# Gated delta rule scan: two steps' triangular inverses in one pass, a state kept in two buffers, and per-head scaling operations

## What is computed

```python
def gated_delta_scan(q, k, v, g, beta, s0):
    ...
    decay = jnp.exp(jnp.where(tril, gcum[..., :, None] - gcum[..., None, :], -jnp.inf))
    kb = kc * bc[..., None]
    lower = jnp.where(strict, jnp.einsum('nbhid,nbhjd->nbhij', kb, kc) * decay, 0.0)
    rhs = jnp.concatenate([vc * bc[..., None], kb * jnp.exp(gcum)[..., None]], axis=-1)
    sol = lax.linalg.triangular_solve(eye + lower, rhs, left_side=True, lower=True, unit_diagonal=True)
    u, w = sol[..., :dv], sol[..., dv:]
    attn = jnp.where(tril, jnp.einsum('nbhid,nbhjd->nbhij', qc, kc) * decay, 0.0)
    def step(S, inp):
        q_i, k_i, u_i, w_i, a_i, g_i = inp
        v_new = u_i - jnp.einsum('bhck,bhkv->bhcv', w_i, S)
        o = (jnp.einsum('bhck,bhkv->bhcv', q_i * jnp.exp(g_i)[..., None], S)
             + jnp.einsum('bhij,bhjv->bhiv', a_i, v_new))
        g_last = g_i[..., -1]
        S = (S * jnp.exp(g_last)[..., None, None]
             + jnp.einsum('bhck,bhcv->bhkv', k_i * jnp.exp(g_last[..., None] - g_i)[..., None], v_new))
        return S, o
```

## Time and profile before

| | us |
|---|---|
| median of 3 runs | 4184.54 (4180.77 to 4185.28) |
| span of the profiled execution | 4178.0 |
| first scan, 214.2 to 418.7 | 204.5 |
| second scan, 574.9 to 776.5 | 201.6 |
| TensorE busy over the span | 3781.0 (90%) |
| VectorE / ScalarE / GpSimd busy | 2122.6 / 870.5 / 398.1 |

### The profile page before, as it was taken

One profiled execution on the slowest core, in us unless ns is written; L12 is line 12 of the kernel. 1 busy time (PEld: TensorE's weight loads), 2 busy tenths in 40 slices (PEclk: granted clock), 3 DMA queues, 4 the chain that ended last, 5 costly groups with the idle time before them and its releaser, 6 DMA issues. The chain is left out here.

```text
span 4178.0 us, 67184 instructions
## 1 busy us (share of the span) xinstructions
PE 3781.0 (90%) x28350; PEld 2477.1 (59%) x28350; DVE 2122.6 (51%) x4187; ACT 870.5 (21%) x2114; POOL 398.1 (10%) x506
## 2 busy tenths in 40 slices
PE   7988989995999979899899598897989999999998
PEld 3477467772444435565677244334358878468877
DVE  3777677555222215576646433333464455564455
ACT  3144134411000002251621100002230001441001
POOL 0033013100111110150600000000000000000000
PEclk9999999997999989899999799998999999999999
DMA  7500520027999971211411799994112222122221
GB/s 250 179 27 12 182 92 18 21 82 278 392 392 393 402 262 41 91 52 41 142 61 61 296 405 405 410 421 156 41 66 81 71 91 96 41 94 93 71 91 56
DMA packets 166940, 674.20 MB, mean 161 GB/s; under 512 B 13480, under 2 KB 26984, under 8 KB 142064
## 3 DMA queue, kind: packets, MB, share of 16 engines
q1 hardware_dynamic: 155232, 650.89, 40.7%
q0 software_dynamic: 9984, 16.78, 1.8%
q10 hardware_dynamic: 1424, 2.23, 0.2%
HBM read 652.85 MB, written 17.02 MB: 160 GB/s over the span
## 5 line engine op out<-in xcount | busy, mean ns | idle before, releaser
L3756 PE MATMUL bank<-weight_ring_extra_b,xs_b 128*32 128x512 f32 x2544 | 281.8, 593 | 2.4 <-DMA weight_ring_extra_b<-in_moe_in 2.4
L3756 PE MATMUL bank<-weight_ring,xs_b 128*32 128x512 f32 x1936 | 219.7, 604 | 11.7 <-DVE xs_b L3859 6.1
L3848 ACT ACTIVATE moe_silu_b<-bank 128x256 f32<-128x256 f32 x80 | 25.5, 383 | 957.5 <-PE bank L3756 957.5
L2865 PE MATMUL bank<-heads_out_b,swiglu_sums_b 128*128 128x256 f32 x1008 | 224.4, 379 | 0.0
L3859 DVE TENSOR_SCALAR xs_b<-bank,factor_b,mod_b 128x64 f32<-128x64 f32 (+1 forms) x384 | 95.4, 323 | 228.3 <-PE bank L3740 228.3
L2865 PEld LDWEIGHTS bank<-heads_out_b,swiglu_sums_b 128*128 128x128 f32 x1008 | 191.5, 190 | 26.0
L3756 PEld LDWEIGHTS bank<-weight_ring_extra_b,xs_b 128*32 128x32 f32 x2544 | 79.1, 110 | 178.4 <-issue 173.3
L3813 PE MATMUL bank<-weight_ring_extra_b,moe_hidT_b 128*32 128x256 f32 x2784 | 161.5, 391 | 12.0 <-DMA weight_ring_extra_b<-in_moe_down 10.4
L1776 POOL TENSOR_TENSOR d_level_b<-d_low_b,d_mask_b 128x256 f32<-128x256 f32 x144 | 115.9, 833 | 544.2 <-DVE d_far_b L2035 542.4
L3900 DVE TENSOR_TENSOR heads_out_b<-heads_out_b,bank 128x256 f32<-128x256 f32 x256 | 90.2, 415 | 151.1 <-PE bank L3793 151.1
L2249 PE MATMUL bank<-hT_b,token_block_sums_b 128*128 128x256 f32 x608 | 145.1, 393 | 15.7 <-DVE hT_b L2383 15.7
(11 more groups left out here) (618 smaller groups left out, 7699.6 us busy)
## 6 DMA issues: line engine op xcount, KB each, us to landing
weight_ring_extra_b<-in_moe_in SPq DMA_DIRECT2D x60, 2048.0 KB, 23.8
weight_ring<-in_moe_in SPq DMA_DIRECT2D x48, 2048.0 KB, 24.5
weight_ring_extra_b<-in_moe_down SPq DMA_DIRECT2D x33, 2048.0 KB, 25.0
weight_ring<-in_ada_w SPq DMA_DIRECT2D x24, 2048.0 KB, 8.1
weight_ring<-in_moe_down SPq DMA_DIRECT2D x21, 2048.0 KB, 25.1
weight_ring<-in_ssd_w_in SPq DMA_DIRECT2D x12, 2048.0 KB, 8.2
hT_b<-in_moe_in SPq DMA_DIRECT2D x10, 2048.0 KB, 41.9
weight_ring<-in_ffn_w_gate SPq DMA_DIRECT2D x10, 2048.0 KB, 7.8
```

Of the source, the lines that this page charges most:

```text
L2865: last = pe.matmul(out, lhs[:, k, :], rhs[:, k, :], start=(k == 0), stop=(k == HK - 1))
L3756: last = pe.matmul(in_bank(g)[lanes[c], :], xs[:, e % 2, kt, g * GROUP:(g + 1) * GROUP], w[:, k, :, c * COLS:(c + 1) * COLS], start=(kt == 0),
L3848: last = act.activation(sl[:, g, :], in_bank(g)[:, 0:COLS], ACT.Silu)
```

## The change

Steps are taken in pairs. Both inverses of a pair are built in one pass: `L`, `far`, `A`, `UW`, `U` and `C` have a further axis `j` for the two steps, and every instruction of a level covers both. At size 64 the transpose is done by 64x64 products with the identity. What is waited for before the pass is now the `L` of both steps, and so their decays and Grams. To find room, slots 0 and 2 of the weight ring are lent to the scan until the last pair's inverse is done (`gdn_lent`), and only then are they loaded for the following stage.

`S` has two buffers, so a step reads the old one while the new one is written, and `state` goes ahead of `o` on TensorE. The right side becomes `V * beta` on GpSimd (`values`) and one scalar_tensor_tensor per head on VectorE (`right`), and the state one scalar_tensor_tensor per head (`renew`). The scaled keys move to ScalarE, by one activation per head (`fade_keys`). All Grams are copied to SBUF and two of each direction are made inside the first pair's levels (sizes 8 and 32).

```diff
+        later = {8: s + 2, 32: s + 3}.get(size, TT)
...
+                pool.tensor_tensor(R[:, d], V[:, t], wide(dec.beta, d, t), ALU.mult).then_inc(pom[d].sem, 1)
...
+                wait(pool, dvm[d], s + 1, "low")
+                pool.tensor_tensor(small(A[:, d, n % 2]), small(L[:, d]), over_small(mask[:, d, n, :]), ALU.mult) \
+                    .then_inc(pom[d].sem, 1)
...
+            for s in PAIRS:
+                invert(s)
+                renew(s)
                 for d in (FWD, BWD):
...
+                    read_out(d, s)
+                    later = gram_at(d, s, SMALL[-1])
+                    wait(pe, acm[d], *((later, "gram") if later else (s, "kend")))
+                    turn_keys(d, s + 1)
+                    read_state(d, s + 1)
+                if more(s):
+                    for d in (FWD, BWD):
+                        wait(pe, acm[d], s + 1, "kend")
+                        scores(d, s + 2)
+                renew(s + 1)
                 for d in (FWD, BWD):
...
+                    read_out(d, s + 1)
...
+                for h in range(GQ):
+                    last = act.activation(KE[:, d, h, :], B[d][0][:, h, :], ACT.Copy,
+                                          scale=dec.to_end[:, t, d, h0 + h:h0 + h + 1])
...
+                for h in range(GQ):
+                    last = dve.scalar_tensor_tensor(out=R[:, d, h, :], in0=B[d][3][:, h, :], scalar=faded[:, t, d, h:h + 1],
+                                                    in1=R[:, d, h, :], op0=ALU.mult, op1=ALU.add)
...
+                for h in range(GQ):
+                    last = dve.scalar_tensor_tensor(out=S[:, d, (s + 1) % 2, h, :], in0=S[:, d, s % 2, h, :],
+                                                    scalar=dec.whole[:, t, d, h0 + h:h0 + h + 1], in1=B[d][3][:, h, :],
+                                                    op0=ALU.mult, op1=ALU.add)
...
             for d in (FWD, BWD):
                 lower(d, 0)
-            for s in steps():
+            for d in (FWD, BWD):
+                attention(d, 0)
+            for d in (FWD, BWD):
+                lower(d, 1)
+            for s in PAIRS:
...
                 for d in (FWD, BWD):
+                    renew(d, s)
+                for d in (FWD, BWD):
+                    if more(s):
+                        lower(d, s + 2)
+                    put_out(d, s)
+                    right(d, s + 1)
+                if more(s):
+                    for d in (FWD, BWD):
+                        attention(d, s + 2)
+                for d in (FWD, BWD):
+                    renew(d, s + 1)
+                for d in (FWD, BWD):
+                    if more(s):
+                        lower(d, s + 3)
+                    put_out(d, s + 1)
```

More of the change, by code:

```diff
@@ L1779, in _, with each @@
         @block.tensor
         def _(pe):
[L1781 removed]
+            def each(d, out, lhsT, rhs):
                 for h in range(GQ):
@@ L2075, in _ @@
+                        level(d, s, size)
+                    if size in (2, 4):
+                        for d in (FWD, BWD):
+                            queries(d, s + size // 4)
+                if not more(s):
                     for d in (FWD, BWD):
-                        beside(d, s, size)
+                        wait(dve, dvm[d], s, f"uv{TOP}")
+                    for name in lent:
+                        dve.sem_inc(core.ring.used_up(name), 1)
                 for d in (FWD, BWD):
-                    t = ORDER[d][s]
```

718 lines of the change are left out of this document (412 added, 306 removed).

## The result

| | kernel before | changed kernel |
|---|---|---|
| median, us | 4184.91 (4 runs, 4180.77 to 4186.46) | 4155.59 (4 runs, 4153.10 to 4160.75) |
| span of the profiled execution, us | 4178.0 | 4153.2 |
| both scans up to the next stage's first matmul, us | 204.96 + 201.83 | 189.22 + 185.44 |

What follows compares the result with a forecast made beforehand. No engine was full; waits between engines set the scans' length. Each scan gains 5.6, 10.1 and 9.7 us in its pairs and loses 12.0 or 10.8 at its start: 28 us, so 4156.5 us, range 4128 to 4190.

Steps and rivals of the forecast that it cites:

- First inverse: Start of each scan: first inverse starts after 24.4 us, 2.0 of it for slow block products; loses 12.0 and 10.8 us.
- Level for two steps: Inverse levels: one level serving two steps takes 4.15 us instead of 2 x 2.55 = 5.1.
- First products to the first transposes: Beginning of a pair's inverse: 8.3 us, with 1.1 more for GpSimd meetings on the inverse's path.
- Two meetings of 0.5 us: Inverse of a pair: VectorE and GpSimd delay each other twice on the path, 1.1 us with rounding.
- Rest: From `new` to the next inverse: TensorE's one queue sets the time, 23.0 us a pair against 27.3.
- Waiting for `R`: At the second `new`: TensorE waits 1.1 us for its second direction.
- Per-head group: VectorE's four per-head operations: 1.06 us a group, bounds 0.96 to 1.64; about six of eight a pair on the path.
- Loads hidden: Scan's end: weight loads into the two lent slots stay hidden; otherwise up to 8 us at each end.
- More overlap: Rival, chance 0.22: GpSimd meetings fall into idle time, per-head groups cost 0.96, starts are 3 us shorter; 4138.5 us.
- VectorE the bound: Rival, chance 0.11: VectorE bounds the stretch between inverses, per-head groups at 1.64 us; no change, 4183.5 us.
- the lock: Rival, chance 0.10: VectorE operations with two SBUF inputs wait for whole GpSimd masks, eight waits a pair; slower, 4209.5 us.
- the clock: Rival, chance 0.05: TensorE's lower clock in every inverse, 10 us a pair; slower, 4216.5 us.

Runs made afterwards that it cites:

- e1: Changed kernel with VectorE's two reads of the transposed size-1 blocks moved ahead of its two reads of GpSimd's mask: 4147.25 us, 0.9923.
- e2: Changed kernel with each GpSimd mask of 128x512 made as two operations of 128x256, one per step: 4150.39 us, 0.9932.
- e12: Changed kernel with fourteen unread 128x128 products a pair on TensorE between turned size-1 blocks and first block product: 4159.45 us, 0.9948.
- e5: Changed kernel with VectorE's per-head operations for right side and state replaced by wide multiplies and adds: 4154.97 us, 0.9930.
- e6: Changed kernel with the scaling of the turned keys moved back from ScalarE to VectorE: 4157.66 us, 0.9945.
- e8: Kernel before with the level of size 16 left out of its inverse: 4150.77 us, 0.9913.
- e3: Changed kernel with the second step's decay in the scaled keys' buffer and the first decay made ahead of the Gram copies: 4145.90 us, 0.9920.
- e7: Changed kernel with the level of size 16 left out of its inverse: 4130.78 us, 0.9876.

## Why the prediction was right, point by point

The mechanism was right: a level for two steps costs less than two levels, the rest is TensorE's queue, and the start pays. That the number came so close (4156.5 forecast, 4155.59 measured) is partly luck, since errors of opposite sign cancel in the inverse and in the sum, as the points show.

- **First inverse, forecast 24.4 us into the scan: 22.50 and 22.85.** The count of the queue (22.4) was right. The 2.0 us that I added for block products at 1.2 GHz fell behind that point, into the first pair (12.16 and 12.31 us to size 4 where others took 9.49 to 11.03). Start and first pair together: 81.8 and 82.3 us, forecast 83.4.
- **Level for two steps, forecast 4.15 us: 3.90, and 4.14 for level 8 with the queries beside it.** Only the latter lies in the 4.1 to 4.3 named as a sign. The chain by ScalarE and VectorE was over-counted: a copy of two halves is 0.66, two subtractions 0.75, where I had 0.72 and 0.8. Three levels took 11.88 (12.8 with the scaled keys), size 32 4.60 (5.0), size 64 3.94 (4.3).
- **First products to the first transposes, forecast 8.3 and about 1.1 for GpSimd, 9.4: 11.01, and 9.49 where the clock held.** At full clock the sum holds to 0.1 us. The term that was mis-sized is the clock, which stood at nothing in the pairs: the lower clock in the block products, which I had placed in the starts alone, came in three of the four later pairs too, for 1.5 us each (e1, e2, e12). "Two meetings of 0.5 us" was short as well. They are 3.10 us for two operations that take 0.68 each, 0.87 a meeting, two thirds more than "1.16 - 0.64", since the mask behind which VectorE waits had grown from 0.73 to 1.27 (e2); at full clock the rest of the sum had room for it. By the Trainium skill ("SBUF — State Buffer", section "SBUF: two separate sides") the second of the two engines waits for the whole operation of the first. e2 agrees in kind: the longest delay falls from 1.07 to 0.52 us with the operation going from 1.27 to 0.73. The rival priced eight whole waits a pair on the path; two meetings, 1.75 us over both directions, are what the rows show at L2245.
- **A pair's inverse, forecast 31.5: 31.43.** The errors of the two points above cancel: +1.6 and -1.7.
- **Rest, forecast 23.0: 22.79. Waiting for `R`, forecast 1.1 us: none between pairs, 0.40 in the last.** TensorE's queue it is. Both times behind the 1.1 were right: TensorE comes to the second `new` 11.7 us after the first (326.05 to 337.78), and the second direction's right side ends after 12.7 (338.71). The reading was not: in that 1.0 us TensorE multiplies for the first direction, which takes 0.9. The sum did not hold the 1.1, so it came out.
- **Per-head group, forecast 1.06: 1.07 to 1.13.** The price was right. "About six of a pair's eight groups lie on the path" stays open: e5's scans grew by 3.8 us in all, but at full clock a pair grew by 2.1.
- **Pairs 54 to 56 us apart: 54.23 and 54.24. First pair, forecast 59.0: 59.29 and 59.44. Last pair, forecast 50.0: 48.91, and 53.20** where the lower clock cost 1.5 us on the way to size 4, 1.0 in size 64 and 1.6 in `new`.
- **Loads hidden:** yes; the stretch between the scans did not grow.
- **Rivals.** More overlap (4138.5) holds for the levels and not for GpSimd; VectorE the bound (4183.5) is not met, and e6 shows what it would look like; the lock (4209.5) acts, with 1.75 us a pair at L2245 where it priced 10.2, and most of that off the path (e1); the clock (4216.5) acts, with 1.5 us in three of four later pairs, some 3 us in the first ones and 4 in one last pair, and not with 10 in each.
- **The sum.** Scans 32.1 us shorter in the traces, forecast 28. The forecast's parts add to 187.9 us a scan, 375.8 for both, and 374.7 were measured; the other 3 us are in the kernel before, whose scans were taken as 403.8 by their steps and are 406.8, one inverse at the lower clock having taken 23.2 us in place of 18.7. The 29.3 of the medians is less, and the profiled spans differ by 24.8: behind the second scan the changed kernel's execution took 3410.9 us and that of before 3401.3, with the same code. That stretch took 3399.7 us (e5) to 3413.5 us (e8) in the other profiled executions, without order by kernel. So the 9.6 us are the spread of single executions, not a price of the change. Here is the other piece of luck: the span was forecast at 4150.0 and was 4153.2, and the 6.5 us added to get the median were 2.4.

## What to carry to other kernels

Serving two problems in one pass of a dependent chain paid here because one problem left the engines idle for much of each round trip: the merged level costs little more than its busiest engine's own work, 3.9 us against 5.1 for two single ones. It costs a longer start, and that is worth its own design: a second buffer for the first two steps gave back 9 of the 19 us that the two starts had grown by. Before moving a wait, ask whether it is on the path: here TensorE's idle time hid behind VectorE's queue, which was the bound that a reordering had to fill, and most of what the first reordering gained was the clock. And compare a stretch between two kernels only at the same granted clock: e5 looks like nothing in the sum of its scans and like 2.1 us a pair at full clock.

## What the runs showed of the hardware

- VectorE's operation with both inputs in SBUF was delayed beside GpSimd by up to most of the length of GpSimd's operation: 0.68 us alone, up to 1.75 beside one of 1.27, up to 1.20 beside one of 0.73. The same operation with an input in PSUM kept its 0.68 beside the same masks (L2249: 0.674 to 0.678 in all twelve). GpSimd can be the one delayed: a mask of 1.27 us took up to 1.84 (changed kernel, L1811).
- TensorE's block products were partly at 1.2 GHz behind two waits of 0.65 and 1.72 us in three of four later pairs of the changed kernel and of e3 and in two of e7's; behind the 1.72 us alone in none of four (e6), and with work in the 1.72 us in none of four (e12).
- The time of a kernel goes with the mean granted clock of its execution: the kernel before, seventeen times on one chip, took 4173.2 us at a mean of 0.967 and 4202.85 at 0.957. A difference of 10 us between single executions says nothing here.
